# Second block: gate projections of the attention branch ahead of the branch's output projection, and the branch's result multiplied by its gate straight out of PSUM

## The chip, the core and the metric

One core of one Trainium2 chip runs the whole program. The time is the device time of one execution in microseconds (us), the median of several runs. Four compute engines matter here: PE (matrix products), DVE (elementwise on vectors), ACT (elementwise, activation functions) and POOL. SP issues the DMAs. Each engine works through its own instructions in order and waits on semaphores for the others.

## What is computed

A model of one sequence of 256 tokens and width 1024. `first_block` has two layers with two feed-forwards each, a pooling mixer and a block attention. `second_block` follows with two branches side by side: a state-space branch (`_ssm_branch`) and a multi-head latent attention (`_mla_branch`). Only the second block is touched:

```python
proj = h @ w_in[l]
u_s, z_s, q_lat, kv_lat, k_rope, z_m, gl_s, gl_m = jnp.split(proj, split_at, axis=-1)
y_s = _ssm_branch(u_s, ...)
glu_a, glu_b = jnp.split(jax.nn.gelu(y_s) @ w_glu[l] + b_glu[l], 2, axis=-1)
y_s = ((glu_a * jax.nn.sigmoid(glu_b)) * jax.nn.silu(z_s)) @ w_br_ssm[l]
y_m = _mla_branch(q_lat, kv_lat, k_rope, positions, ...)
y_m = (y_m * jax.nn.silu(z_m)) @ w_br_mla[l]
merged = jax.nn.sigmoid(gl_s) * y_s + jax.nn.sigmoid(gl_m) * y_m
out = merged @ w_out[l]
x = x + gate[:, None] * _rmsnorm(out, g_post[l])
```

All of it is float32.

## The kernel before

**Weights come as a stream of units.** A unit is 128 partitions by 1024 floats, 512 KB: for a projection, the weights of 128 output columns. `PHASES` gives the order of the 391 units, and the host lays them out in DRAM in that order (`parts`). Each unit goes through four hands: SP loads it into one of four `land` slots (`load_unit`), ACT rounds it to the upper part `w_hi` (`split_hi`, L392), DVE takes the lower part `w_lo` as a difference (`split_lo`, L396), and PE multiplies. A full float32 product is three PE products per 128 rows: `w_hi` by the upper input, `w_hi` by the lower, `w_lo` by the upper (`products`, L404 to L406; 24 per unit and 256 tokens). `w_hi` and `w_lo` have four slots each, so ACT can round unit u only when PE has finished unit u - 4 (semaphore `used`).

**Results come out in two PSUM banks.** `column_unit` writes result tile o into `tiles[:, o % 2]`, and first waits (`wait_bank`) until the owner of tile o - 2 has taken that tile out. `TILES` names the owner of each tile: "a" is ACT, "d" is DVE. Owners count up `freed["a"]` or `freed["d"]`.

**The gate stretch** is the list `GATES`: 32 units that only project, in four groups of eight. Before, these are `zs` (steps 0 to 7: silu of z_s into `zs_t`), `brm` (8 to 15: the attention branch's output projection, copied into `mrg`), `glm` (16 to 23: sigmoid of gl_m into `gs_t`) and `gls` (24 to 31: sigmoid of gl_s into the same `gs_t`). I call them steps 0 to 31, and PE, ACT and DVE each have one loop over them:

- PE: `column_unit` of step i. After steps 2, 5 and 10 it also does `state_in` (the inputs of the state-space scan), and after steps 8, 14, 20 and 26 two calls of `state_out` (L1074, L1076), each time for one more pair of the eight groups of channels.
- ACT: takes out tile i (`evacuate`, L1270), then `ahead()` rounds the unit of step i + 4. After the `state_out` steps it computes the gelu of the two results (`gelu_tile`, L1501), and at steps 19 and 26 it rounds what has come back from DRAM (`gelu_hi`, L1505).
- DVE: `ahead()` splits the unit of step i + 4, in `glm` steps multiplies `mrg[:, n]` by `gs_t[:, n]` (L2178, both in SBUF), and at most steps has one of 16 parts of the scan (`ssm_part`). Per pair k of groups there are four parts: part 0 (L2139 to L2144: four products that read PSUM, then two sums within SBUF), parts 1 and 2 (L2149: eight scans each), part 3 (L2156 to L2161), which ends with `zz_done`. `state_out` of pair k waits for that `zz_done`. Pairs 0, 1, 2 and 3 end their part 3 in the DVE steps 6, 12, 18 and 24; PE asks for them after its steps 8, 14, 20 and 26.
- POOL: after `zz_done` of pairs 0 and 1 it builds a table of rotations for pairs 2 and 3 (`table_step`, six products L2237 to L2242).

A change of activation function may need another function table in ACT (ACT_TABLE_LOAD). Before the gate stretch ACT computes a silu over all of `zm` (L1494). After it follow the `glu`, `brs` and `out` phases; in `brs`, DVE multiplies each result straight out of PSUM by `gs_t[:, n]` (L2201) and adds `mrg`.

## Time and profile before

| what | us |
|---|---|
| median of 3 runs | 1294.92 |
| lowest and highest run | 1294.7, 1297.7 |
| the profiled execution, its own time | 1294.78 |
| its span, first to last instruction | 1292.9 |
| in the span: gate stretch on PE, steps 0 to 31 | 1070.4 to 1188.6 |
| PE busy (share of the span) | 1234.9 (96%) |
| DVE busy | 1084.9 (84%) |
| ACT busy | 670.6 (52%) |
| POOL busy | 167.1 (13%) |

The profiled execution took 1294.78 us, 1.9 us more than its span; what lies outside the span is launch and end. Its time is 0.1 us below the median. All times of rows are us from the start of the span. A row of the timeline has the start, the length, the engine, the line, the operation, what is written from what, and the count; in brackets stands how long the engine was idle before and what released it. Instructions of one engine overlap a little at their ends, so what one adds to a queue is the distance between starts, not its length.

### The profile page before, as it was taken

To read this page: it belongs to the slowest core of one execution; us is meant where nothing else is said; L and a number is where in the kernel's file an instruction comes from. 1 tells how busy PE (TensorE), PEld (TensorE's weight loads), DVE (VectorE), ACT (ScalarE), POOL (GpSimd) and SP (SyncE) were. 2 spreads that over 40 slices of the span, in tenths; PEclk is the share of its full clock that TensorE was granted. 3 is DMA by queue.
4 is the path that set the end of the run, shared out by engine and by line. 5 is a ranking of instruction groups with operands and counts; after the bars stand their busy time and mean duration, and the time that the engine had idled before them with its cause. 6 is when DMAs were issued, how large, how long until landed. Compare 5 with 4: busy or idle time off the path is not lost.

```text
span 1292.9 us, 26721 instructions
## 1 busy us (share of the span) xinstructions
PE 1234.9 (96%) x10504; PEld 1205.2 (93%) x10504; DVE 1084.9 (84%) x1673; ACT 670.6 (52%) x1130; POOL 167.1 (13%) x195
## 2 busy tenths in 40 slices
PE   2999999899999999999999999999999999999996
PEld 1999999799999988999999999999999989999996
DVE  6998988898888877989989788999987577995584
ACT  2543434554444555664457664444465665455453
POOL 4599900000000000000001000000000022410000
PEclk8999999999999999999999999999999999999999
DMA  9999887489888459988853399887665898555561
GB/s 362 385 332 320 309 318 271 168 309 327 311 315 292 146 194 361 322 313 308 316 202 115 115 311 323 299 305 247 215 196 180 135 154 185 160 163 182 181 194 50
DMA packets 110926, 319.75 MB, mean 247 GB/s; under 512 B 24096, under 2 KB 35808, under 8 KB 110560
## 3 DMA queue, kind: packets, MB, share of 16 engines
q1 hardware_dynamic: 110816, 318.23, 74.0%
q8 instruction: 75, 1.23, 0.4%
q14 instruction: 35, 0.29, 0.1%
HBM read 313.18 MB, written 5.01 MB: 246 GB/s over the span
## 4 chain that ended last, share of the span: by engine, by line
PE 78%; DVE 12%; ACT 3%; DMA 3%; issue 2%; SPq 2%; ACTq 0%; DVEq 0%
PE quad L404 16%; PE quad L406 16%; PE quad L405 16%; PE acc L404 8%; PE acc L406 7%; PE acc L405 7%; DVE w_lo L396 3%; DVE arena L1572 2%; ACT w_hi L392 1%; PE quad L581 1%; PE quad L607 1%; DMA arena<-in_ssm_bw 1%; PE quad L609 1%; DMA land<-in_stream 1%; DMA x<-in_x_t 1%
## 5 line engine op out<-in xcount | busy, mean ns | idle before, releaser
L392 ACT CAST w_hi<-land 128x1024 fp32r<-128x1024 f32 x391 | 409.4, 1049 | 352.3 <-PE quad L406 239.3
L396 DVE TENSOR_TENSOR w_lo<-land,w_hi 128x1024 fp32r<-128x1024 f32 x391 | 485.1, 1246 | 118.5 <-ACT w_hi L392 116.2
L404 PE MATMUL quad<-xs_hi,w_hi 128*128 128x256 f32 (+1 forms) x1384 | 391.9, 283 | 0.8 <-DVE arena L2101 0.5
L406 PE MATMUL quad<-xs_hi,w_lo 128*128 128x256 f32 (+1 forms) x1384 | 390.0, 282 | 0.0
L405 PE MATMUL quad<-xs_lo,w_hi 128*128 128x256 f32 (+1 forms) x1384 | 389.4, 281 | 0.0
L404 PEld LDWEIGHTS quad<-xs_hi,w_hi 128*128 128x128 f32 x1384 | 260.8, 188 | 3.1 <-issue 0.9
L405 PEld LDWEIGHTS quad<-xs_lo,w_hi 128*128 128x128 f32 x1384 | 261.8, 189 | 0.1
L406 PEld LDWEIGHTS quad<-xs_hi,w_lo 128*128 128x128 f32 x1384 | 261.3, 189 | 0.0
L1572 DVE SCALAR_TENSOR_TENSOR arena<-arena 128x1024 f32<-128x1024 f32 x184 | 226.8, 1239 | 11.9 <-ACT arena L1295 8.4
L404 PE MATMUL acc<-h_hi,w_hi 128*128 128x256 f32 x704 | 196.9, 280 | 1.7 <-DVE h_lo L1622 1.3
L406 PE MATMUL acc<-h_hi,w_lo 128*128 128x256 f32 x704 | 196.7, 279 | 0.0
L405 PE MATMUL acc<-h_lo,w_hi 128*128 128x256 f32 x704 | 196.5, 279 | 0.0
L404 PE MATMUL quad<-as_hi,w_hi 128*128 128x258 f32 (+1 forms) x648 | 184.1, 284 | 1.2 <-DVE arena L2089 0.8
L406 PE MATMUL quad<-as_hi,w_lo 128*128 128x258 f32 (+1 forms) x648 | 182.1, 281 | 0.0
L405 PE MATMUL quad<-as_lo,w_hi 128*128 128x258 f32 (+1 forms) x648 | 182.0, 281 | 0.0
L404 PEld LDWEIGHTS acc<-h_hi,w_hi 128*128 128x128 f32 x704 | 132.2, 188 | 2.4 <-DVE w_lo L396 1.9
L406 PEld LDWEIGHTS acc<-h_hi,w_lo 128*128 128x128 f32 x704 | 132.4, 188 | 0.0
L405 PEld LDWEIGHTS acc<-h_lo,w_hi 128*128 128x128 f32 x704 | 132.3, 188 | 0.0
L404 PEld LDWEIGHTS quad<-as_hi,w_hi 128*128 128x128 f32 x648 | 122.3, 189 | 2.1 <-ACT arena L1270 0.7
L405 PEld LDWEIGHTS quad<-as_lo,w_hi 128*128 128x128 f32 x648 | 122.6, 189 | 0.1
L406 PEld LDWEIGHTS quad<-as_hi,w_lo 128*128 128x128 f32 x648 | 122.2, 189 | 0.0
L2329 POOL TENSOR_TENSOR arena<-arena,cons 128x256 f32<-128x256 f32 x8 | 6.6, 826 | 547.4 <-ACT arena L1359 545.7
(356 smaller groups left out, 1622.3 us busy)
## 6 DMA issues: line engine op xcount, KB each, us to landing
land<-in_stream SPq DMA_DIRECT2D x391, 512.0 KB, 4.4
arena<-in_gstream SPq DMA_DIRECT2D x184, 512.0 KB, 6.2
w_dram<-arena SPq DMA_DIRECT2D x3, 512.0 KB, 5.5
arena<-w_dram SPq DMA_DIRECT2D x6, 256.0 KB, 11.0
arena<-in_c_rows SPq DMA_DIRECT2D x2, 512.0 KB, 5.3
x<-in_x_t SPq DMA_DIRECT2D x1, 1024.0 KB, 9.5
arena<-in_ssm_bn SPq DMA_DIRECT2D x1, 1024.0 KB, 5.3
u_dram<-arena SPq DMA_DIRECT2D x1, 1024.0 KB, 5.3
```

Of the source, the lines that this page charges most:

```text
L392: nc.scalar.copy(w_hi[:, u % RING], land[:, u % LAND]).then_inc(hi_done, 1)
L396: nc.vector.tensor_tensor(w_lo[:, u % RING], land[:, u % LAND], w_hi[:, u % RING].bitcast(F32), ALU.subtract).then_inc(lo_done, 1)
L404: nc.tensor.matmul(outs, lh, rh, start=first, stop=False, **kw)
L405: nc.tensor.matmul(outs, lh, rl, start=False, stop=False, **kw)
L406: last = nc.tensor.matmul(outs, ll, rh, start=False, stop=end, **kw)
L581: m = nc.tensor.matmul(nrm[:, 0:T], ones, t_buf[:, k], start=(k == 0), stop=(k == KT - 1))
L607: nc.tensor.matmul(outs[c], lh, hi[:, k], start=(k == 0 and c in fresh), stop=False, skip_group_check=True)
L609: nc.tensor.matmul(outs[c], ll, hi[:, k], start=False, stop=False, skip_group_check=True)
L1572: V.scalar_tensor_tensor(out=rows, in0=rows, scalar=1.0, in1=c_rows[vector], op0=ALU.mult, op1=ALU.mult, accum_out=mods[:, bass.ds(i * 8 + ...
L2329: G.tensor_tensor(q_cos[:, h % 2], qT[:, h], cos1, ALU.mult).then_inc(q_cosd, 1)
```

## The change

The four groups of the gate stretch are put in the order `glm`, `brm`, `zs`, `gls`. The sigmoid of gl_m is now ready before the attention branch's results come, and these are no longer copied by ACT: their tiles belong to DVE, which multiplies them out of PSUM by `gs_t` into `mrg`. The separate product in the `glm` steps is gone, its semaphore `glm_done` too. `gls` writes `gs_t` again once DVE has freed the `brm` tile of the same number. `zs_t` and `gs_t` change places in SBUF, since `zm` is still being read when `glm` begins. The weight stream on the host is reordered to match; SP's, POOL's and PE's instructions are the same but for the semaphore that PE waits for before some tiles.

```diff
-          ("lat", 4), ("kr", 1), ("u", 6), ("qup", 4), ("kvup", 4), ("u2", 2), ("zm", 8), ("zs", 8), ("brm", 8),
-          ("glm", 8), ("gls", 8), ("glu", 16), ("brs", 8), ("out", 8)]
+          ("lat", 4), ("kr", 1), ("u", 6), ("qup", 4), ("kvup", 4), ("u2", 2), ("zm", 8), ("glm", 8), ("brm", 8),
+          ("zs", 8), ("gls", 8), ("glu", 16), ("brs", 8), ("out", 8)]
...
-         ("u", 6, "a"), ("qup", 8, "d"), ("kvup", 12, "a"), ("u2", 2, "a"), ("att2+zm", 16, "x"), ("zs", 8, "a"),
-         ("brm", 8, "a"), ("glm", 8, "a"), ("gls", 8, "a"), ("glu", 16, "y"), ("brs", 8, "d"), ("out", 8, "a")]
+         ("u", 6, "a"), ("qup", 8, "d"), ("kvup", 12, "a"), ("u2", 2, "a"), ("att2+zm", 16, "x"), ("glm", 8, "a"),
+         ("brm", 8, "d"), ("zs", 8, "a"), ("gls", 8, "a"), ("glu", 16, "y"), ("brs", 8, "d"), ("out", 8, "a")]
...
-GATES = [(_name, _n) for _name in ("zs", "brm", "glm", "gls") for _n in range(KT)]
+GATES = [(_name, _n) for _name in ("glm", "brm", "zs", "gls") for _n in range(KT)]
...
-        zs_t = region(40, [KT, T])
+        zs_t = region(16, [KT, T])
         mrg = region(48, [KT, T])
-        gs_t = region(16, [KT, T])
+        gs_t = region(40, [KT, T])
...
                 if nm == "zs":
                     evacuate(o, tile_of(nm, n), zs_t[:, n], ACT.Silu)
-                elif nm == "brm":
-                    evacuate(o, tile_of(nm, n), mrg[:, n])
-                else:
+                elif nm != "brm":
                     if nm == "gls":
-                        act.wait_ge(glm_done, n + 1)
+                        wait_freed(act, TILE["brm"] + n)
                     evacuate(o, tile_of(nm, n), gs_t[:, n], ACT.Sigmoid)
                 ahead()
...
             for i, (nm, n) in enumerate(GATES):
+                if nm == "brm":
+                    wait_tile(dve, TILE["brm"] + n)
+                    wait_freed(dve, TILE["glm"] + n)
+                    V.tensor_tensor(mrg[:, n], tiles[:, (TILE["brm"] + n) % 2, 0:T], gs_t[:, n],
+                                    ALU.mult).then_inc(freed["d"], 1)
                 ahead()
...
-                if nm == "glm":
-                    wait_freed(dve, TILE["glm"] + n)
-                    V.tensor_tensor(mrg[:, n], mrg[:, n], gs_t[:, n], ALU.mult).then_inc(glm_done, 1)
```

ACT at the start of the gate stretch and from step 24 on. L1270 is `evacuate`, L392 `split_hi`, L1494 the silu over `zm`:

```order
 L1494 ACT_TABLE_LOAD
 L1494 ACTIVATE arena<-arena 128x8x256 [waits freed_a]
+L1270 ACT_TABLE_LOAD
 L1270 ACTIVATE arena<-quad 128x256 [waits used]
 L392 CAST w_hi<-land 128x1024 [waits used,landed3]
```

A table load has come in behind the silu, since step 0 is a sigmoid now.

```order
-L1270 ACTIVATE arena<-quad 128x256 [waits used,glm_done]
-L392 CAST w_hi<-land 128x1024 [waits used,landed3]
...
+L1270 ACT_TABLE_LOAD [waits used]
+L1270 ACTIVATE arena<-quad 128x256 [waits freed_d]
+L392 CAST w_hi<-land 128x1024 [waits used,landed3]
```

At step 24 (silu to sigmoid, the first `gls` tile) a table load has come in that itself waits for PE's tile.

DVE, steps 13 to 16, before. L396 is `split_lo`, L2139 to L2144 part 0 of pair 2, L2149 scans, L2178 the product within SBUF:

```order
L2161 TENSOR_TENSOR arena<-arena 128x8x63
L396 TENSOR_TENSOR w_lo<-land,w_hi 128x1024 [waits hi_done] x2
L2139 TENSOR_TENSOR arena<-acc4,rope_tab 128x512 [waits bu_done,tab_done,zz_done]
...
L2144 TENSOR_TENSOR arena<-arena 128x512
L396 TENSOR_TENSOR w_lo<-land,w_hi 128x1024 [waits hi_done,dve_s]
L2149 SCALAR_TENSOR_TENSOR arena<-ssm_s,arena 128x64 x8
L396 TENSOR_TENSOR w_lo<-land,w_hi 128x1024 [waits hi_done,dve_s]
L2178 TENSOR_TENSOR arena<-arena 128x256 [waits freed_a]
```

No product stands here before step 16. And after (lines are 2 lower; L2173 is the new product out of PSUM):

```order
L2159 TENSOR_TENSOR arena<-arena 128x8x63
L2173 TENSOR_TENSOR arena<-quad,arena 128x256 [waits freed_a,used]
L396 TENSOR_TENSOR w_lo<-land,w_hi 128x1024 [waits hi_done]
L2173 TENSOR_TENSOR arena<-quad,arena 128x256 [waits freed_a,used]
L396 TENSOR_TENSOR w_lo<-land,w_hi 128x1024 [waits hi_done]
L2137 TENSOR_TENSOR arena<-acc4,rope_tab 128x512 [waits bu_done,tab_done,zz_done]
...
L2142 TENSOR_TENSOR arena<-arena 128x512
L2173 TENSOR_TENSOR arena<-quad,arena 128x256 [waits freed_a,used,dve_s]
L396 TENSOR_TENSOR w_lo<-land,w_hi 128x1024 [waits hi_done]
L2147 SCALAR_TENSOR_TENSOR arena<-ssm_s,arena 128x64 x8
```

Three products now stand in steps 13, 14 and 15, each ahead of the split of its step; the one of step 15 stands behind the whole of part 0. From step 16 on there is none.

## Rows read from the trace of the kernel before

**Rows 1.** The page: busy time by engine (1) and the chain that ended last (4).

```profile
PE 1234.9 (96%) x10504; PEld 1205.2 (93%) x10504; DVE 1084.9 (84%) x1673; ACT 670.6 (52%) x1130; POOL 167.1 (13%) x195
...
PE 78%; DVE 12%; ACT 3%; DMA 3%; issue 2%; SPq 2%; ACTq 0%; DVEq 0%
```

**Rows 2.** Windows: us, busy us (count) of PE, PEld, DVE, ACT, POOL, PEclk, DMA share, GB/s.

```profile
1097.00:1150.00 53.00, 49.78 (x606) 48.83 (x606) 49.67 (x86) 26.20 (x41) 18.51 (x12) 1.00 0.56 169
```

**Rows 3.** Waits of 1095 to 1195: who <- releaser: us in total, times, longest.

```profile
ACT arena L1270 <- PE quad L406: 43.5, 25, 3.7
...
PE quad L1074 <- DVE arena L2161: 4.1, 4, 1.7
```

**Rows 4.** Timeline, PE, first product of pairs 2, 3: start, us, what, [idle <-releaser].

```profile
1149.56 0.27 PE L1074 MATMUL quad<-arena 64*64 64x64 f32 x1 [1.67 <-DVE arena L2161]
...
1170.94 0.27 PE L1074 MATMUL quad<-arena 64*64 64x64 f32 x1 [0.91 <-DVE arena L2161]
```

**Rows 5.** Timeline, ACT, steps 0 and 1 of the gate stretch.

```profile
1070.40 1.28 ACT L1494 ACT_TABLE_LOAD   x1
1071.69 1.92 ACT L1494 ACTIVATE arena<-arena 128x2048 f32<-128x2048 f32 x1
1073.52 0.38 ACT L1270 ACTIVATE arena<-quad 128x256 f32<-128x256 f32 x1
1080.63 1.04 ACT L392 CAST w_hi<-land 128x1024 fp32r<-128x1024 f32 x1 [6.72 <-DMA land<-in_stream]
```

**Rows 6.** Timeline, ACT, steps 12 and 16.

```profile
1120.98 0.39 ACT L1270 ACTIVATE arena<-quad 128x256 f32<-128x256 f32 x1 [1.55 <-PE quad L406]
1121.26 1.04 ACT L392 CAST w_hi<-land 128x1024 fp32r<-128x1024 f32 x1
...
1136.51 0.39 ACT L1270 ACTIVATE arena<-quad 128x256 f32<-128x256 f32 x1 [0.24 <-PE quad L406]
```

**Rows 7.** Timeline, DVE, steps 12 to 17.

```profile
1122.40 1.23 DVE L396 TENSOR_TENSOR w_lo<-land,w_hi 128x1024 fp32r<-128x1024 f32 x1 [0.24 <-ACT w_hi L392]
...
1126.66 0.68 DVE L2161 TENSOR_TENSOR arena<-arena 128x504 f32<-128x504 f32 x1
1127.25 3.23 DVE L396 TENSOR_TENSOR w_lo<-land,w_hi 128x1024 fp32r<-128x1024 f32 x2
...
1132.90 1.57 DVE L2143 TENSOR_TENSOR arena<-arena 128x512 f32<-128x512 f32 x1
1134.40 1.56 DVE L2144 TENSOR_TENSOR arena<-arena 128x512 f32<-128x512 f32 x1
1135.99 2.19 DVE L396 TENSOR_TENSOR w_lo<-land,w_hi 128x1024 fp32r<-128x1024 f32 x1
...
1139.69 1.23 DVE L396 TENSOR_TENSOR w_lo<-land,w_hi 128x1024 fp32r<-128x1024 f32 x1
1140.84 0.42 DVE L2178 TENSOR_TENSOR arena<-arena 128x256 f32<-128x256 f32 x1
1141.17 1.22 DVE L396 TENSOR_TENSOR w_lo<-land,w_hi 128x1024 fp32r<-128x1024 f32 x1
```

**Rows 8.** Timeline, POOL, first and fourth of the six table products.

```profile
1127.47 1.92 POOL L2237 TENSOR_TENSOR cons<-base_t,chunk_t 128x512 f32<-128x512 f32 x1 [14.00 <-DVE arena L2161]
...
1132.86 1.07 POOL L2240 TENSOR_TENSOR cons<-base_t,chunk_t 128x512 f32<-128x512 f32 x1
```

**Rows 9.** Line L2201, a product that reads PSUM: count, min/median/max ns, first and last start.

```profile
L2201 DVE TENSOR_TENSOR arena<-quad,arena x8: 414/424/425, 1239.9 to 1257.7; 128x256 f32<-128x256 f32 x8
```

**Rows 10.** Timeline, ACT, step 24.

```profile
1164.43 0.39 ACT L1270 ACTIVATE arena<-quad 128x256 f32<-128x256 f32 x1 [1.59 <-PE quad L406]
1164.71 1.04 ACT L392 CAST w_hi<-land 128x1024 fp32r<-128x1024 f32 x1
```

**Rows 11.** Timeline, DVE, step 24.

```profile
1165.96 1.23 DVE L396 TENSOR_TENSOR w_lo<-land,w_hi 128x1024 fp32r<-128x1024 f32 x1
```

**Rows 12.** Timeline, ACT, step 27.

```profile
1177.25 1.28 ACT L1270 ACT_TABLE_LOAD   x1 [1.71 <-PE quad L406]
```

More of the change, by code:

```diff
@@ L341, in build_program @@
         y_done, gel_done, gv_done = sem("y_done"), sem("gel_done"), sem("gv_done")
-        zm_done, glm_done = sem("zm_done"), sem("glm_done")
+        zm_done = sem("zm_done")
         zero_cols = sem("zero_cols")
@@ L537, in _ @@
                     sp.dma_start(u2[r:r + 16], u_rows[g, t]).then_inc(u_in, 16)
-            for u in range(UNIT["zm"] + 6, UNIT["zs"] + 4):
+            for u in range(UNIT["zm"] + 6, UNIT["glm"] + 4):
                 load_unit(sp, u, u % LAND)
@@ L547, in _ @@
                     sp.dma_start(ba2[r:r + 16].rearrange("p j r n -> p j (r n)"), w_rows[g]).then_inc(ba_in, 16)
-            u = UNIT["zs"] + 4
+            u = UNIT["glm"] + 4
             for k in range(4):
-                while u < UNIT["zs"] + Y_AT[k] + 8:
+                while u < UNIT["glm"] + Y_AT[k] + 8:
                     load_unit(sp, u, u % LAND)
@@ L2443 @@
         columns(w_in2[:, 2592:3616]),
+        columns(w_in2[:, 4640:5664]),
+        columns(a["w_br_mla_2"][0]),
         columns(w_in2[:, 1024:2048]),
-        columns(a["w_br_mla_2"][0]),
-        columns(w_in2[:, 4640:5664]),
         columns(w_in2[:, 3616:4640]),
```

## The prediction

> **What bounds the kernel now.** I read the page first: PE is busy for 96% of the span, and the chain that ended last runs through PE for 78% and DVE for 12% [rows 1]. So a change of elementwise work can win only where PE stands still. The windows put the change's place, steps 6 to 20, at 53 us in which PE is busy for 49.8 and DVE for 49.7 [rows 2]: here DVE is as full as PE. The waits then say who waits: ACT's evacuations wait for PE, 43.5 us in total, so ACT has room; PE waits for DVE in four places, 4.1 us in total, always for L2161, the end of part 3 of the scan [rows 3]. The longest two are before `state_out` of pairs 2 and 3, 1.67 and 0.91 us [rows 4]. That is the whole prize in the gate stretch. Even if all four waits went, 4.1 us is 0.32% of 1294.9; 0.3% (3.9 us) is about what a measurement of this kernel can tell from no change.
>
> **Eight copies off ACT.** Each was an evacuation of 0.39 us, which takes 0.28 us of ACT's queue (1120.98 to 1121.26) [rows 6]. ACT waits 1.55 us for PE ahead of it [rows 6], so by itself this gives nothing. What it does give: in steps 8 to 15 the rounding of the next unit starts as soon as PE is done, 0.28 us sooner. That counts only where DVE sits waiting for it. It does in step 12, where DVE's split starts at 1122.40 after 0.24 us of idling [rows 7]: that wait goes (see below).
>
> **A table load at step 0.** The silu over `zm` ends at 1073.5, the evacuation of tile 0 follows at 1073.52, and the rounding behind it waits 6.72 us for its unit's DMA until 1080.63 [rows 5]. A load of 1.28 us moves the evacuation to 1074.8. PE needs that bank for step 2, two units after its start of step 0 at 1070.4; a unit is 2.87 us of ACT's cycle (1.55 + 0.28 + 1.04 [rows 6]) when PE sets the pace, so at 1076.1. Cost 0; the cover is 1.3 us. Without it the price would be at most 1.28 us.
>
> **Eight products, from steps 16 to 23 to steps 8 to 15.** The new one reads PSUM. The nearest row is L2201, the same form: 424 ns [rows 9], against 0.42 for the old one within SBUF, which takes 0.33 us of the queue (1140.84 to 1141.17) [rows 7]. I take 0.33 for both. The Trainium skill (VectorE: DVE Perf Modes, the section on the TRN2 errata) gives a DVE operation that reads PSUM 120 fixed cycles against 58, which speaks against this change by 0.065 us an operation, an estimate from that page, 0.2 to 0.3 us in sum; the rows show 0.006, and they decide.
>
> Steps 8 to 11: DVE has idle time before step 12, so these four are free. In step 12 I put the queue together anew: DVE was free at 1122.16 (1122.40 less 0.24) and is so 0.28 earlier, since it waited for ACT in step 11 too: 1121.9. The product takes 0.33, the rounding is done by 1122.0 (1121.26 + 1.04 - 0.28), the split starts at 1122.2. Part 3 of pair 1 ends 0.2 us sooner: **-0.2** at the wait before pair 1, carried down DVE's queue.
>
> Steps 13 to 15: DVE now runs without a pause to step 20, so three more products add 3 x 0.33 = 1.0 us; steps 16, 17 and 18 lose three, -1.0. On paper that cancels before part 3 of pair 2. But here POOL is in the way. Its table products start 0.14 us behind L2161, the first takes 1.92 us where the fourth, while DVE reads PSUM, takes 1.07 [rows 8], and DVE's operations with both inputs in SBUF take 1.57, 1.56 and 2.19 us where they otherwise take 0.68 (L2161, nearly the size of the first two) and 1.23 [rows 7]: the two take turns, whole operations at a time, while DVE's PSUM readers pass freely (in the 2.4 us between the two splits, which end at 1130.5, and L2143 at 1132.90 there are four of them, 0.60 each). Before, a split began at 1127.25 and was first; now a product out of PSUM stands there, POOL gets its turn first, and the split waits for it. Turn by turn, at 1.1 us for POOL's and for a split, 0.6 for L2143 and L2144: POOL to 1128.3, split to 1129.4, product, POOL to 1130.4, split to 1131.5, four PSUM readers beside POOL to 1133.9; there DVE and POOL come within 0.1 us of each other. If L2143 is first it ends at 1134.6, POOL goes to 1135.7, and L2144 ends at 1136.3; if POOL is first, both start about one turn later, and L2144 ends at 1137.6. Before it was 1135.95. The product of step 15 stands behind it and frees its bank at 1136.6 to 1137.9. PE wants that bank for step 17, after tile 16, which is done at 1136.4 [rows 6] less the 0.2 won. **A new wait of PE, 0.4 to 1.7 us, before step 17.** Queued behind the product in DVE: the split for step 19, the scans, part 3 of pair 2.
>
> That wait is mostly covered, for PE waited 1.67 us for the same DVE queue before pair 2 anyway [rows 4]. If part 0 ends early (1136.3), DVE arrives up to 0.5 sooner at pair 2 than before; if it ends late (1137.6), the roundings of steps 17 and 18 (they need PE's tiles 17 and 18) also come late and DVE waits for them: up to 0.5 later. I take **0**, from -0.5 to +0.5, for the moment at which `state_out` of pair 2 starts (1149.56). Everything before it, the -0.2 included, is in that figure.
>
> **A table load at step 24.** Between pair 2 and pair 3 DVE loses five products, 1.65 us, and PE's wait before pair 3 was 0.91 [rows 4]. That looks like a gain. But at step 24 DVE started its split at 1165.96, and the rounding it needs had ended only at 1165.75 (1164.71 + 1.04) [rows 10, 11]. So DVE was 0.2 us from being bound by ACT, and a faster DVE gains 0.2 at most. And ACT now has the new load in just that place: after `zs` (silu) comes the first `gls` (sigmoid), and the order shows that the load itself waits for PE's tile. Step 27, where such a load stood already, shows it: 1.71 us of waiting for PE, and then 1.28 us of load in front of the evacuation [rows 12]. So evacuation, rounding, split and part 3 all shift by 1.28: rounding done at 1167.03, split at 1167.1 and not 1165.96, **+1.1 us** on PE's wait before pair 3 (0.91 becomes 2.0). Bounds: -0.2 if the load were hidden, +1.28. I take +1.1, since the rows around it leave no other order. Nothing later gives it back: the gelu results of pair 3 go through DRAM and are rounded after step 31, in ACT's order, and from there PE is busy without a gap.
>
> For the load the Trainium skill has a rule that speaks against the change (ScalarE: Activation LUTs, What ACT_TABLE_LOAD costs): 1283 ns of load plus about 1380 ns of drain, so one should group functions by table set. The row at 1070.40 shows 1.28, and the next activation starts 1.29 us later [rows 5]: no drain. By the rule the load at step 24 would cost 2.66, an estimate from that page.
>
> **Sum.** 0 (step 0) + 0 (up to pair 2) + 1.1 (pair 3) = +1.1 us. The span goes from 1292.9 to 1294.0, the profiled execution from 1294.78 to 1295.9. It was 0.1 below the median, so the median goes from 1294.92 to **1296.0**.
>
> **Rivals.**
> A, *the load is hidden and the products pay*: DVE saves its five products and the 0.5 of the early end of part 0; PE's waits before pairs 2 and 3 shrink by 0.5 and 0.2: -0.7, 1294.2. For it: DVE is the releaser in all four waits. Against: the load stands in the chain of step 24.
> B, *it does nothing*: the copies and products were beside PE's work, and DVE and ACT trade equal parts: 1294.9. For it: 96% busy PE. Against: the same load.
> C, *slower by a feedback*: call X the end of the product of step 15. PE's tile 17 ends at X + 2.9, tile 18 at X + 5.7; its rounding is done 1.4 later, DVE's split 1.2 after that and part 3 of pair 2 another 3.7: pair 2 can start at X + 12.0. Up to X = 1137.6 this is no later than the 1149.56 of before, so PE's new wait costs nothing in the end; past it every us counts in full. If POOL gets two turns more than I count (1.3 us), X is 1139.2 and the price +1.6: with the load +2.7, 1297.6. From X = 1140.4 on it is slower by over 0.3%: 2.8 + 1.1 = +3.9, 1298.8. For it: DVE is full from 1122.4 on [rows 2, 7]. Against: POOL has six products in all.
> D, *the load costs more than its row*: the activation behind it starts late by as much as the load takes, another 1.28 [rows 12] on top of 1.1 at step 24: 1297.3. Against: the load at 1070.40, whose activation starts 1.29 later [rows 5]. The page's rule above is this rival, with 1.38 for the 1.28.
>
> **Chances.** Forecast, between +0.4 and +1.9: 0.62. A 0.10, B 0.12, C 0.12 (a third of it past 0.3%), D 0.04. The range reaches from just below A to the middle of C: 1293.9 to 1298.3. Faster by over 0.3% would need 3.9 us out of 4.1 of waits: 0.02. Slower by over 0.3%: 0.05, from C. Within: 0.93.
>
> **What would show it.** In the profile of the changed kernel: PE's idle times before pairs 0 and 1 together 0.2 below the 1.5 of now (4.1 less 1.67 less 0.91); a PE row at step 17 that waits for L2173; less than 1.67 before pair 2, with its start within 0.5 of 1149.56; an ACT_TABLE_LOAD at step 24 with an idle time before it, released by PE; about 2.0 us before pair 3. I am wrong if the stretch from pair 2 to pair 3 grows by less than 0.5 us, if PE waits at any step 9 to 16 for a bank, or if the time moves by more than 3 us either way.

## The result, and the profile after

| | kernel before | changed kernel |
|---|---|---|
| median, 11 runs each | 1295.07 | 1299.80 |
| lowest and highest run | 1293.46, 1297.70 | 1296.67, 1302.69 |
| profiled execution, its own time | 1294.78 | 1299.19 |
| its span | 1292.9 | 1297.4 |

The ratio is 1.0032, with a 95% interval of 1.0022 to 1.0042: 4.2 us by the ratio, 4.7 by the two medians. The forecast of 1296.0 is too low by 3.8 us, and its range ended at 1298.3. A repetition (below) gave 1.0022.

The page of the changed kernel, engines and chain, to lay beside [rows 1]:

```profile
PE 1237.9 (95%) x10504; PEld 1208.0 (93%) x10504; DVE 1084.5 (84%) x1673; ACT 671.2 (52%) x1124; POOL 167.5 (13%) x195
...
PE 82%; DVE 10%; ACT 3%; issue 2%; DMA 2%; SPq 1%; ACTq 0%; DVEq 0%
```

PE is busy 3.0 us longer with the same 10504 products, so some of them ran slower. The windows say where (us, busy us and count of PE, PEld, DVE, ACT and POOL, then PEclk, DMA share, GB/s). First the changed kernel, then the kernel before:

```profile
440.00:450.00 10.00, 7.83 (x51) 7.81 (x52) 9.19 (x20) 6.06 (x16) 0.00 (x0) 0.83 0.35 109
1053.00:1059.00 6.00, 6.00 (x40) 5.80 (x37) 4.68 (x9) 2.80 (x10) 0.00 (x0) 0.72 0.36 122
1097.00:1153.00 56.00, 52.43 (x625) 51.28 (x625) 52.69 (x94) 23.02 (x32) 18.20 (x12) 1.00 0.56 166
```

```profile
440.00:450.00 10.00, 8.13 (x61) 7.85 (x62) 8.89 (x20) 6.12 (x16) 0.00 (x0) 1.00 0.34 109
1053.00:1059.00 6.00, 6.00 (x50) 5.31 (x49) 5.24 (x10) 3.88 (x11) 0.85 (x1) 1.00 0.40 119
```

The granted clock is 0.83 over ten us in the one and 1.00 in the other: 1.7 us of full clock are missing, in a part of the program that the change doesn't touch. The same happens at 1053. I call such a stretch, in which TensorE has 1.2 and not 2.4 GHz, a **half-clock piece**; 1.7 us missing at half clock is a piece of 3.4 us. In the gate stretch itself the clock is 1.00 in both [rows 2].

Because of these pieces the starts of the two traces can't be compared; distances can. The first product of each `state_out` pair, and PE's wait at step 17, in the changed kernel (the line of part 3's end is L2159 now), to lay beside [rows 4]:

```profile
1106.36 0.30 PE L1074 MATMUL quad<-arena 64*64 64x64 f32 x2 [0.82 <-DVE arena L2159]
```

```profile
1129.79 0.32 PE L1074 MATMUL quad<-arena 64*64 64x64 f32 x2 [0.63 <-DVE arena L2159]
```

```profile
1140.24 0.39 PE L404 MATMUL quad<-xs_hi,w_hi 128*128 128x256 f32 x1 [1.38 <-DVE arena L2173]
```

```profile
1152.65 0.32 PE L1074 MATMUL quad<-arena 64*64 64x64 f32 x2 [0.74 <-DVE arena L2159]
```

```profile
1175.21 0.33 PE L1074 MATMUL quad<-arena 64*64 64x64 f32 x2 [2.07 <-DVE arena L2159]
```

| distance between pairs, us | before | changed | difference |
|---|---|---|---|
| 0 to 1 | 23.52 | 23.43 | -0.09 |
| 1 to 2 | 22.17 | 22.86 | +0.69 |
| 2 to 3 | 21.38 | 22.56 | +1.18 |
| sum | 67.07 | 68.85 | +1.78 |

In two traces of each kernel these distances agree within 0.1 us. So the stretch costs **1.8 us**, not 1.1; and the medians show more than that. The spans of the two traces differ by 4.5 us: 2.5 lie ahead of pair 0, where the two pieces are, 1.8 between pairs 0 and 3, and 0.2 behind pair 3.

**Pair 3.** ACT from step 24 on, and the DVE split behind it, to lay beside [rows 10 to 12]:

```profile
1167.51 1.28 ACT L1270 ACT_TABLE_LOAD   x1 [1.57 <-PE quad L406]
1168.81 0.39 ACT L1270 ACTIVATE arena<-quad 128x256 f32<-128x256 f32 x1
1169.09 1.04 ACT L392 CAST w_hi<-land 128x1024 fp32r<-128x1024 f32 x1
```

```profile
1170.23 1.23 DVE L396 TENSOR_TENSOR w_lo<-land,w_hi 128x1024 fp32r<-128x1024 f32 x1 [1.56 <-ACT w_hi L392]
```

The load waits for PE, then stands ahead of evacuation and rounding, and DVE waits 1.56 us for the rounding. This is the forecast chain, row by row.

**Pair 2.** DVE from step 13 to 18 (L2173 is the product out of PSUM, L2141 and L2142 the sums of part 0, [rows 7]) and POOL's first two products [rows 8]:

```profile
1129.65 0.41 DVE L2173 TENSOR_TENSOR arena<-quad,arena 128x256 f32<-128x256 f32 x1
1129.99 2.04 DVE L396 TENSOR_TENSOR w_lo<-land,w_hi 128x1024 fp32r<-128x1024 f32 x1
1131.95 0.41 DVE L2173 TENSOR_TENSOR arena<-quad,arena 128x256 f32<-128x256 f32 x1
1132.28 1.75 DVE L396 TENSOR_TENSOR w_lo<-land,w_hi 128x1024 fp32r<-128x1024 f32 x1
...
1136.46 1.58 DVE L2141 TENSOR_TENSOR arena<-arena 128x512 f32<-128x512 f32 x1
1137.96 1.76 DVE L2142 TENSOR_TENSOR arena<-arena 128x512 f32<-128x512 f32 x1
1139.76 0.42 DVE L2173 TENSOR_TENSOR arena<-quad,arena 128x256 f32<-128x256 f32 x1
...
1144.75 1.23 DVE L396 TENSOR_TENSOR w_lo<-land,w_hi 128x1024 fp32r<-128x1024 f32 x1 [0.69 <-ACT w_hi L392]
...
1147.67 1.22 DVE L396 TENSOR_TENSOR w_lo<-land,w_hi 128x1024 fp32r<-128x1024 f32 x1 [0.22 <-ACT w_hi L392]
```

```profile
1129.88 1.07 POOL L2237 TENSOR_TENSOR cons<-base_t,chunk_t 128x512 f32<-128x512 f32 x1 [13.90 <-DVE arena L2159]
1131.03 1.93 POOL L2238 TENSOR_TENSOR rh<-base_t,chunk_t 128x512 f32<-128x512 f32 x1
```

POOL starts at 1129.88 and the split at 1129.99: POOL is first, as expected, and the split takes 2.04 us. The product of step 15 ends at 1140.18, PE's tile 17 starts at 1140.24 after 1.38 us of waiting. Then comes what the sum put at zero: DVE waits 0.69 and 0.22 us for the roundings of steps 17 and 18, which came late since PE's tiles did.

**Step 0.** ACT's load and evacuation, and the rounding that waits for its DMA, [rows 5]:

```profile
1076.58 1.28 ACT L1270 ACT_TABLE_LOAD   x1
1077.87 0.39 ACT L1270 ACTIVATE arena<-quad 128x256 f32<-128x256 f32 x1
1082.83 1.04 ACT L392 CAST w_hi<-land 128x1024 fp32r<-128x1024 f32 x1 [4.57 <-DMA land<-in_stream]
```

The load is covered: the wait for the DMA is 4.57 and not 6.72 us. The next instruction starts 1.29 us after it, so rival D falls here, and at step 24 (1167.51 to 1168.81) as well.

### The profile page after: what moved, and what is told of

Read it like the earlier page. It is cut to its first block, busy times and chain, and to the rows that moved or that the text cites. A ratio compares the mean times of both kernels' runs of the same rounds, so it can differ in the third digit from the quotient of the medians.

```text
span 1297.4 us, 26719 instructions
## 1 busy us (share of the span) xinstructions
PE 1237.9 (95%) x10504; PEld 1208.0 (93%) x10504; DVE 1084.5 (84%) x1673; ACT 671.2 (52%) x1124; POOL 167.5 (13%) x195
## 4 chain that ended last, share of the span: by engine, by line
PE 82%; DVE 10%; ACT 3%; issue 2%; DMA 2%; SPq 1%; ACTq 0%; DVEq 0%
PE quad L404 17%; PE quad L406 17%; PE quad L405 17%; PE acc L404 8%; PE acc L406 7%; PE acc L405 7%; DVE w_lo L396 3%; DVE arena L1570 2%; ACT w_hi L392 1%; PE quad L607 1%; PE quad L609 1%; PE quad L581 1%; DMA land<-in_stream 1%; DMA x<-in_x_t 1%; DVE x L1692 1%
## 5 line engine op out<-in xcount | busy, mean ns | idle before, releaser
L392 ACT CAST w_hi<-land 128x1024 fp32r<-128x1024 f32 x391 | 409.4, 1049 | 368.7 <-PE quad L406 250.1
L396 DVE TENSOR_TENSOR w_lo<-land,w_hi 128x1024 fp32r<-128x1024 f32 x391 | 484.1, 1243 | 120.2 <-ACT w_hi L392 117.9
```

Source lines behind the costliest of these rows:

```text
L392: nc.scalar.copy(w_hi[:, u % RING], land[:, u % LAND]).then_inc(hi_done, 1)
L396: nc.vector.tensor_tensor(w_lo[:, u % RING], land[:, u % LAND], w_hi[:, u % RING].bitcast(F32), ALU.subtract).then_inc(lo_done, 1)
```

## Experiments

All were timed in five rounds beside runs of the kernel before on the same chip. "Mean" is the difference of the means to that kernel in the same comparison (single runs scatter with a standard deviation of 1.7 us, so a mean of 12 runs is good to about 0.5 us); "clock" is the mean granted clock of the runs, that of the kernel before being 0.9909 to 0.9916; "sum" is the distance from pair 0 to pair 3.

| kernel | runs | ratio, 95% interval | mean, us | clock | sum, us |
|---|---|---|---|---|---|
| rep_before | 12 | 1.0003 (0.9993 to 1.0013) | +0.1 | 0.9917 | 67.07 |
| rep_after | 12 | 1.0022 (1.0011 to 1.0034) | +2.3 | 0.9908 | 68.77 |
| a_nowait | 12 | 1.0004 (0.9991 to 1.0016) | +0.9 | 0.9913 | 67.52 |
| a_actcopy | 8 | 1.0027 (1.0016 to 1.0038) | +3.2 | 0.9903 | 68.49 |
| a_fill | 11 | 1.0006 (0.9994 to 1.0018) | +0.5 | 0.9914 | 68.91 |
| b_delay | 12 | 1.0005 (0.9994 to 1.0015) | +0.9 | 0.9908 | 68.33 |
| b_defer | 12 | 0.9990 (0.9978 to 1.0003) | -1.2 | 0.9913 | 65.97 |
| b_delay2 | 12 | 1.0027 (1.0014 to 1.0041) | +4.0 | 0.9903 | 69.73 |
| b_delay2_fill | 11 | 1.0013 (1.0002 to 1.0025) | +2.1 | 0.9916 | 69.71 |
| b_early | 11 | 1.0023 (1.0012 to 1.0034) | +2.5 | 0.9908 | 66.97 |
| b_best | 11 | 1.0016 (1.0005 to 1.0027) | +2.0 | 0.9917 | 65.96 |
| b_defer_fill | 12 | 1.0004 (0.9991 to 1.0018) | +0.6 | 0.9909 | 66.05 |
| b_fill442 | 12 | 0.9978 (0.9966 to 0.9989) | -2.7 | 0.9926 | 67.00 |
| b_defer442 | 6 | 0.9965 (0.9952 to 0.9978) | -3.4 | 0.9920 | 66.03 |
| a_442 | 12 | 1.0010 (0.9999 to 1.0021) | +1.1 | 0.9920 | 68.84 |
| a_442_fill | 12 | 0.9996 (0.9986 to 1.0007) | -0.2 | 0.9928 | 68.85 |

There were six comparisons, each with its own runs of the kernel before: rep_before to a_actcopy; a_fill to b_defer; b_delay2 to b_best; b_defer_fill; b_fill442 and b_defer442; a_442 and a_442_fill.

### Both kernels again (rep_before, rep_after)

> The kernel before, once more, for a second trace and for its spread beside the kernel after on one chip. Theory T1 (the change itself costs 1.8 us in the gate stretch, 1.38 before step 17 partly covered and 1.2 before pair 3; the other 2.5 us of the two traces lie ahead of the gate stretch in code that is the same, where TensorE ran at half clock for 443 to 447 and 1053 to 1059 us in the trace of after and not in that of before, and that is chance of a run): the distance from state_out of pair 0 to that of pair 3 is again 67.1 us, while the arrival at pair 0 (1103.9) may move by 2 us or more. Theory T2 (the half-clock pieces come with the changed kernel): no such pieces here, arrival within 0.5 us of 1103.9.

> The changed kernel, once more. Both theories: pair 0 to pair 3 again 68.9 us. T1: the half-clock pieces near 443 and 1053 us are there or not by chance, arrival at pair 0 between 1103.5 and 1108, ratio to before 1.001 to 1.003. T2: both pieces are there again, arrival at 1106.4, ratio 1.003 to 1.004.

The kernel before against itself is 1.0003. The changed one is 1.0022 and not 1.0032: of the 4.2 us that the ratio of the first comparison gives, some 1 to 2 were chance. Over all runs, 23 of the changed kernel have a mean of 1299.35 at a clock of 0.9905, 163 of the kernel before in the later comparisons 1296.49 at 0.9914: **2.9 us**, give or take 0.9. The stretch explains 1.8 of them. Among the 163 runs of the kernel before a run is 1.1 us longer for each 0.001 that its clock is lower; by that slope the clock of the changed kernel, 0.0009 lower, is worth 1.0. That slope is a correlation, and the mean clock is no pure count of pieces: it also holds the half clock at the start of the span, which lasts 10.2 us in 11 of the 18 traces and 13.7 in seven, whatever the kernel. What is left to find is why the clock of the changed kernel is lower.

### Without the wait that holds the table load (a_nowait)

```diff
-                    if nm == "gls":
-                        wait_freed(act, TILE["brm"] + n)
```

> The changed kernel without ACT's wait for the freed brm tile before each gls tile (PE's order already implies it), so that the table load of step 24 carries no wait and can be done while ACT idles ahead of PE's tile. If the load in the chain makes the 1.18 us between pairs 2 and 3: that distance falls from 22.56 to 21.3 (21.38 before), PE's wait before pair 3 from 2.07 to 0.7 or less, and the time is 1.2 us below that of the changed kernel. Rival (DVE or the DMAs make it, not the load): the distance stays at 22.5 and the time does not move.

The sigmoid's instruction then has one wait (for PE), and the load in front of it none. ACT at step 24 in a_nowait:

```profile
1164.76 1.28 ACT L1270 ACT_TABLE_LOAD   x1
1166.27 0.38 ACT L1270 ACTIVATE arena<-quad 128x256 f32<-128x256 f32 x1 [0.23 <-PE quad L406]
```

The load runs while ACT would wait for PE. The distance from pair 2 to pair 3 is 21.23 us, 1.33 shorter than in the changed kernel and even 0.15 shorter than before. So the load makes the whole +1.18 of pair 3, and only since it stands behind the wait.

### Copies by ACT, products within SBUF, in the new order (a_actcopy)

```diff
-("brm", 8, "d")
+("brm", 8, "a")
...
+                elif nm == "brm":
+                    evacuate(o, tile_of(nm, n), mrg[:, n])
...
-                    V.tensor_tensor(mrg[:, n], tiles[:, (TILE["brm"] + n) % 2, 0:T], gs_t[:, n],
-                                    ALU.mult).then_inc(freed["d"], 1)
+                    V.tensor_tensor(mrg[:, n], mrg[:, n], gs_t[:, n], ALU.mult).then_inc(glm_done, 1)
```

> The changed kernel with the brm tiles copied out by ACT again, as before, and multiplied by DVE within SBUF in the same steps 8 to 15: the new order, without a PSUM bank held by DVE. If the held bank makes the loss between pairs 1 and 2 (22.86 against 22.17): PE's wait of 1.38 before step 17 goes, and the distance falls to 22.2 to 22.5. Rival (DVE's longer queue beside POOL makes it, and the bank only shows it): the wait before step 17 goes, but the wait before pair 2 grows by as much and the distance stays at 22.8. The load at step 24 stays, so pair 2 to pair 3 is 22.5 in both.

DVE in steps 14 and 15 of a_actcopy, and PE at pair 2:

```profile
1131.61 1.28 DVE L2174 TENSOR_TENSOR arena<-arena 128x256 f32<-128x256 f32 x1
...
1139.75 0.43 DVE L2174 TENSOR_TENSOR arena<-arena 128x256 f32<-128x256 f32 x1
```

```profile
1151.67 0.33 PE L1074 MATMUL quad<-arena 64*64 64x64 f32 x2 [1.75 <-DVE arena L2161]
```

The product within SBUF waits in turn with POOL (1.28 us; out of PSUM the one in its place took 0.41), and the product of step 15 comes just as late in DVE's queue (1139.75, that is 10.36 us after pair 1 starts on PE; in the changed kernel 9.97). But it holds no bank now. PE doesn't wait at step 17, waits 1.75 before pair 2 as before, and the distance from pair 1 to 2 is 22.28, 0.11 above before. So of the 0.69 of pair 2, 0.58 comes from the **held bank**: a late product delays PE's tile, this the rounding, this DVE. DVE being late is not enough. This counts from pair 1. That pair itself comes 0.13 us later than before in a_actcopy and 0.09 sooner in the changed kernel; from pair 0 to pair 2 a_actcopy is 0.24 us longer than before and the changed kernel 0.60, so that the bank's share is 0.36 there. The mean of a_actcopy doesn't show this gain (+3.2 against +2.3), which is within the scatter of eight and twelve runs.

That a two-input operation within SBUF takes turns with POOL and a reader of PSUM does not is what the Trainium skill says (SBUF — State Buffer, Who interferes with whom: the shared port pair is an exclusive lock, and issue order decides who blocks); the rows agree, 1.28 against 0.41.

### Products deferred (b_defer)

```diff
+MERGE_AT = {19: (0,), 20: (1,), 21: (2,), 25: (3, 4, 5, 6, 7)}
...
-                if nm == "glm":
-                    wait_freed(dve, TILE["glm"] + n)
-                    V.tensor_tensor(mrg[:, n], mrg[:, n], gs_t[:, n], ALU.mult).then_inc(glm_done, 1)
+                for m in MERGE_AT.get(i, ()):
+                    wait_freed(dve, TILE["glm"] + m)
+                    V.tensor_tensor(mrg[:, m], mrg[:, m], gs_t[:, m], ALU.mult).then_inc(glm_done, 1)
```

> The kernel before (old order, ACT copies) with DVE's eight products moved within the glm and gls steps: products 0, 1, 2 in steps 19, 20, 21, products 3 to 7 in step 25, behind part 3 of pair 3, where DVE idles for 6.7 us. If DVE's queue is what PE waits for at pair 2 and ACT's rounding what it waits for at pair 3: pair 1 to pair 2 falls from 22.17 to 21.2, pair 2 to pair 3 from 21.38 to 21.2, so -1.2 in all, and the time is 1.2 to 2 us below before. Rival: PE's own work fills the stretch, and the distances fall by less than 0.3.

This is the kernel before, with the products taken out of DVE's way to pair 2 only. PE at pairs 2 and 3 in b_defer:

```profile
1150.54 0.32 PE L1075 MATMUL quad<-arena 64*64 64x64 f32 x2 [0.75 <-DVE arena L2162]
```

```profile
1171.83 0.33 PE L1075 MATMUL quad<-arena 64*64 64x64 f32 x2 [0.80 <-DVE arena L2162]
```

The wait before pair 2 falls from 1.67 to 0.75 and the sum by 1.1 us, as expected. In the times that is 0.9990, which can't be told from no change by itself.

### Does a long wait before pair 3 bring half-clock pieces? (a_fill, b_delay, b_delay2, b_delay2_fill)

a_fill is the changed kernel with useless products in the wait before pair 3, b_delay the kernel before with two DVE products of part 3 of pair 3 done twice:

```diff
+                if f >= 2:
+                    pe.wait_ge(gel_done, f - 1)
+                if f == 6:
+                    for _ in range(8):
+                        nc.tensor.matmul(y_out[0][:, 0:P], ones, ident, start=True, stop=True)
                 if f % 2 == 0:
                     pe.wait_ge(zz_done, f // 2 + 1)
-                if f >= 2:
-                    pe.wait_ge(gel_done, f - 1)
```

The wait for `gel_done` moves ahead of the useless products, since they write where the results of the pair before stood; so it does in the other kernels with this filler.

```diff
+                    if k == 3:
+                        V.tensor_tensor(m0, v[:, 1], sn, ALU.mult)
+                        link(V.tensor_tensor(m1, v[:, 1], cs, ALU.mult))
```

> The changed kernel with eight useless 128-column float32 products on TensorE after step 26, while it would wait for pair 3 (their result is overwritten). The wait of about 2.07 us becomes work; the distances between the pairs stay (22.56 from pair 2 to pair 3). T1 (the change costs the 1.8 us of the distances, the rest is chance): the mean time stays that of the changed kernel, the mean granted clock 0.9905. T3 (a wait of over 2 us before pair 3 makes TensorE fall to half clock in some runs, near 1174 us as in the trace of a_actcopy): the mean clock goes up towards 0.9915 and the mean time falls by 1 us or more without a change in the distances.

> The kernel before with two products of part 3 of pair 3 done twice on DVE (the same values), some 1.2 to 1.3 us more in front of pair 3 and nothing else: the size of the loss that the table load of step 24 makes. T1: pair 2 to pair 3 goes from 21.38 to 22.6, PE's wait from 0.9 to 2.1, the mean time by +1.2, the mean clock stays at 0.9916. T3: the same distances, the mean time by +2 to +3, the mean clock to 0.991 or less, since some runs have a piece at half clock behind the longer wait.

a_fill shows the sum of the changed kernel without its excess; its mean is even 1.3 us less than the sum asks for, which the pieces behind pair 3 can't explain. b_delay's sum is 1.26 us longer and its mean +0.9, where +2 to +3 was expected with pieces and +1.2 without: no excess that could be told, though its trace has a half-clock piece behind pair 3. As this was unclear, the delay was doubled (b_delay2: three times each product) and put on the chip together with the same kernel with 15 fillers (b_delay2_fill).

> The kernel before, with the first two products of part 3 of pair 3 done three times (four more products of 0.68 us on VectorE, nothing left out). In b_delay two more products made the distance from pair 2 to pair 3 1.33 us longer, so here it should be 2.7 longer (24.1) and PE's wait before pair 3 about 3.6 us. If only the wait itself costs (theory W), the mean is 2.7 us above the kernel before of this call. If a wait past 2 us is in addition followed by a piece in which TensorE has the clock of 1.2 GHz (theory T3), such a piece stands behind pair 3 in the trace, the mean is 3.5 to 4.7 above, and the mean granted clock is below that of the kernel before by 0.0005 or more.

> b_delay2 with 15 useless products of 128 columns on PE ahead of the wait before pair 3 (0.22 us each by a_fill, 3.3 us together), which keep PE busy through most of the wait. The distance from pair 2 to pair 3 should be that of b_delay2 within 0.1 us. Theory W: the same mean as b_delay2 within 0.5 us and no difference in the clock. Theory T3: no piece at the low clock behind pair 3, mean 0.8 to 2 us below b_delay2, and the clock of the kernel before.

PE and its window behind pair 3, first b_delay2, then b_delay2_fill (L1067 is the filler):

```profile
1175.39 0.33 PE L1074 MATMUL quad<-arena 64*64 64x64 f32 x2 [3.55 <-DVE arena L2164]
```

```profile
1174.00:1180.00 6.00, 4.61 (x97) 4.50 (x97) 3.56 (x5) 0.95 (x3) 0.00 (x0) 0.73 0.30 90
```

```profile
1171.90 3.51 PE L1067 MATMUL quad<-cons 128*128 128x128 f32 x30
1175.61 0.32 PE L1076 MATMUL quad<-arena 64*64 64x64 f32 x2 [0.20 <-DVE arena L2166]
```

```profile
1174.00:1180.00 6.00, 5.79 (x119) 5.54 (x118) 3.79 (x5) 2.33 (x5) 0.00 (x0) 1.00 0.25 90
```

Both have the same sum within 0.02 us, so by the stretch alone they are equal. The one in which PE stands idle for 3.55 us has a PEclk of 0.73 behind it; the one in which PE is kept busy has 1.00, and its mean is 1.9 us lower and its clock 0.0013 higher.

What a piece costs there can be read from all 18 traces. From the start of pair 3 to the end of the span it is 121.97 to 122.21 us in the 14 traces without a piece behind pair 3, and 123.48 to 123.76 in the four with one (a_actcopy, b_delay, b_delay2, a_442): **1.3 to 1.8 us** a piece.

### The filler near 442 (b_fill442, b_defer442, a_442, a_442_fill)

Half-clock pieces near 442 stand in 9 of the 14 traces of kernels without a filler there, always at one idle time of PE, here in the changed kernel:

```profile
442.17 0.36 PE L607 MATMUL quad<-as_hi,w_hi 128*128 128x258 f32 x1 [2.56 <-DVE w_lo L396]
```

```diff
                 pe.wait_ge(shift_cols, 2 * (e + 1))
+                for _ in range(9 if f == 2 else 0):
+                    nc.tensor.matmul(quad[:, 0, 0:P], ones, ident, start=True, stop=True)
                 first_units(head_unit(f, 0), [quad[:, b, 0:T + 2] for b in range(3)], *late_in[f], KT * stage,
```

> The kernel before with 9 useless products of 128 columns on PE in the wait of 2.55 us that ends near 442 (in b_defer_fill 9 such products took 2.25 us, but stood at 246, behind another wait). Nothing is left out. Theory I (the idle time brings the pieces at 1.2 GHz): none near 442, mean granted clock above that of the kernel before by 0.0006 to 0.0012, mean 0.8 to 1.5 us below. Theory O (they come from elsewhere): a piece near 442 as often as before, same mean within 0.5 us. In both the wait before the products at 442 is 0.3 us or less.

> b_fill442 with the products of b_defer (the eight products behind each other's scans, distances from pair 0 to pair 3 of 66.0 us in sum and not 67.1). Theory I: 1.9 to 2.6 us below the kernel before of this call, ratio 0.998 to 0.9985. Theory O: 0.6 to 1.6 us below.

PE and the window in b_fill442 (L713 is the filler):

```profile
440.01 2.17 PE L713 MATMUL quad<-cons 128*128 128x128 f32 x18
442.52 0.39 PE L607 MATMUL quad<-as_hi,w_hi 128*128 128x258 f32 x1 [0.34 <-DVE w_lo L396]
```

```profile
440.00:450.00 10.00, 9.66 (x76) 9.29 (x75) 9.75 (x22) 6.62 (x18) 0.00 (x0) 1.00 0.38 129
```

None of the four kernels with this filler has a half-clock piece there. It does no useful work and makes the kernel **2.7 us faster** (1.4 to 4.4 by the interval). With b_defer's edit on top (b_defer442) the ratio is 0.9965: this version beats both kernels. The traces explain less. Eight splits of DVE lie across this wait (from its 133rd to its 141st): they take 33.4 to 33.7 us in the nine traces with a piece, 32.1 to 32.2 in the five without, and 31.9 to 32.0 with the filler. So a piece costs 1.3 to 1.6 us, 9 of 14 of that is 1.0, and the filler gives 0.2 more. The other pairs that differ by this filler alone, from different comparisons, give 2.2 (b_defer442 and b_defer), 1.2 (a_442 and rep_after) and 0.7 us (a_442_fill and a_fill); all four together 1.9, give or take 0.8. What is above 1.2 isn't explained, and may be chance.

> The changed kernel with the 9 useless products of b_fill442 in the wait near 442. b_fill442 gained 2.7 us on the mean of the kernel before; the same here. Against the kernel before of this call: -2.7, +1.8 for the distances (total 68.8), and by theory T3 (a piece at 1.2 GHz behind the wait of 2.07 us in some runs) another +0.5 to +1.3: mean -0.4 to +0.4. If the rest was chance (theory W): mean -0.9 within 0.5. Mean clock by T3 below the 0.9926 of b_fill442 by 0.0004 or more, by W the same.

> a_442 with the 8 useless products of a_fill ahead of the wait before pair 3, distances as in a_442 within 0.1 us. Theory T3: mean 0.5 to 1.3 us below a_442 and a clock above it by 0.0004 or more; theory W: the same mean and clock. Both: -0.9 against the kernel before of this call, no piece at 1.2 GHz behind 1170.

a_442 and a_442_fill are the changed kernel with that filler, without and with the one of a_fill. Their windows behind pair 3:

```profile
1174.00:1180.00 6.00, 6.00 (x108) 5.93 (x105) 1.55 (x2) 1.76 (x4) 0.00 (x0) 0.76 0.36 98
```

```profile
1174.00:1180.00 6.00, 6.00 (x98) 5.93 (x95) 0.95 (x1) 2.73 (x5) 0.00 (x0) 1.00 0.44 122
```

At sums of 68.84 and 68.85 the means differ by 1.2 us and the clocks by 0.0008, as expected with pieces; both means are some 0.7 us above what was expected, in keeping with the filler near 442 giving less than 2.7. Taken with the other two pairs of the same kind (b_delay2 and b_delay2_fill 1.9; rep_after and a_fill, from two comparisons, 2.3 less 0.5), keeping PE busy in the wait before pair 3 gives 1.6 us, give or take 0.8. Against b_fill442, which has the same filler near 442, a_442_fill is 2.6 us longer and a_442 3.8, with 1.8 from the sum: of the 2.0 us of a_442 above the stretch, the filler before pair 3 takes away 1.2, within a scatter of about 1 us. In the traces, of six with a wait of 2.07 us or more before pair 3 four have a half-clock piece behind it (a_actcopy, b_delay, b_delay2, a_442; not the first trace of the changed kernel nor rep_after's); of twelve with less, none. Four of six at some 1.5 us a piece would be 1.0 us on the average.

### Two attempts that failed (b_early; b_best, b_defer_fill)

Another idle time, one that varies, stands in the attention, near 1051 (L796, PE waits for ACT's copy L1291). ACT's queue ahead of it in rep_before, then in b_defer, and PE there in b_defer:

```profile
1045.74 1.05 ACT L392 CAST w_hi<-land 128x1024 fp32r<-128x1024 f32 x1 [2.43 <-DMA land<-in_stream]
```

```profile
1048.28 1.04 ACT L393 CAST w_hi<-land 128x1024 fp32r<-128x1024 f32 x1 [4.46 <-DMA land<-in_stream]
```

```profile
1051.91 0.52 PE L797 MATMUL quad<-arena 128*64 128x256 f32 x2 [2.09 <-ACT arena L1292]
```

A rounding stands in front of ACT's exponentials and waits for weights that land now earlier, now later; PE waits 0 to 2.1 us, by chance. Behind waits of 1.88 to 2.10 a half-clock piece followed in five traces of six, behind shorter ones in none. b_early moves that rounding behind the copy:

```diff
-                if g:
-                    ahead()
+                if g:
+                    ahead({3: 0, 4: 2}.get(g, 1))
```

> The kernel before, with one rounding of the attention moved: the cast that waits for its weights from DRAM ahead of the exponentials of group 5 (2.4 to 4.5 us in nine traces, by chance) now comes behind the copy of group 4. Nothing is left out. In the traces PE's wait at L796 near 1051 was 0 to 2.1 us, the later that transfer landed the longer, and a piece at the low clock of TensorE followed in four of the five traces with a wait of 1.88 us or more. Theory S (this is one source of the spread between runs): the wait at L796 near 1051 is gone, the mean is 0.5 to 2.5 us below the kernel before and the standard deviation of the runs below its 1.7 us. Theory O (the spread comes from elsewhere): same mean within 0.5 us, same spread.

DVE and PE in b_early:

```profile
1050.31 1.23 DVE L396 TENSOR_TENSOR w_lo<-land,w_hi 128x1024 fp32r<-128x1024 f32 x1 [4.02 <-ACT w_hi L392]
```

```profile
1057.53 0.44 PE L796 MATMUL quad<-arena 128*64 128x256 f32 x2 [2.18 <-ACT arena L1291]
```

The wait near 1051 is gone, and one of 2.18 us stands at the next group: DVE now waits 4.02 us for the postponed rounding, with the maxima of the scores queued behind its split. The mean is 2.5 us worse, where 0.5 to 2.5 better was expected. The theory of the spread isn't refuted, but the edit only moved the wait. No half-clock piece follows the wait of 2.18, here or in b_best, so it doesn't explain the loss.

> The kernel before with three edits, nothing left out: the products of b_defer, the rounding of b_early, and 9 useless products of 128 columns on PE in its wait of 2.55 us near 440 (one of the places where a piece at 1.2 GHz followed in some traces). By b_defer -1.1 us (total of the distances from pair 0 to pair 3 66.0, not 67.1), by b_early 0.5 to 2.5, by the filler 0 to 1: mean 1.6 to 4.6 us below the kernel before, and no low clock near 442 in the trace. If the pieces near 442 don't come from the idle time ahead of them, they are seen here as often as elsewhere (four of nine traces) and the gain stays at 1.6 to 3.6.

> b_defer (the kernel before with its eight products behind each other's scans, steps 19 to 25) and the 9 useless products of 128 columns on PE in the wait of 2.55 us near 440, without the moved rounding of b_best; nothing is left out. In twelve traces of kernels without this filler a piece at 1.2 GHz followed near 442 in eight, in the one with it in none. A piece costs 1.5 to 2 us, so if the idle time is what brings it, the filler gains about 1.2 us on the mean of the runs: with the 1.1 of b_defer the mean is 1.5 to 3 us below the kernel before of this call, ratio 0.998 to 0.999, and the mean granted clock above its. If the pieces come from elsewhere, the mean is that of b_defer, 0.3 to 1.3 us below.

Both put the nine fillers into the wrong place, `f == 1` for `f == 2`. They stand behind a wait of 0.62 us at 246, as b_defer_fill shows, and the wait near 442 was left as it was, so the expectation of b_defer_fill, where it says "in the one with it in none", counts a trace of b_best in which that wait was not filled:

```profile
246.32 2.25 PE L714 MATMUL quad<-cons 128*128 128x128 f32 x18 [0.62 <-DVE x L1697]
```

So they measure b_defer plus 2.25 us of useless work in PE's way, and b_best in addition b_early's loss. That would be +1.0 and +3.6; measured are +0.6, in keeping with it, and +2.0, which is 1.6 less; they say nothing on the fillers near 442, which is why b_fill442 followed.

## Why the prediction was wrong

**Pairs 0 and 1: right in sign.** The waits before them are 1.45 together and not 1.55: 0.1 less, where 0.2 was expected.

**The held bank: right, and its price missed.** The new wait at step 17 is 1.38 us (0.4 to 1.7 expected), by the mechanism and the order of turns that the working called the late case. The step that failed is "I take **0**, from -0.5 to +0.5" for the start of `state_out` of pair 2: it is +0.6 from pair 0 on, +0.69 from pair 1. Rival C had the formula, pair 2 at X + 12.0. X is 1140.18, which is 1137.8 in the trace of before (pair 1 started 2.40 earlier there), and pair 2 started at X + 12.5. Half a us too little in a chain of roundings and splits, and the late case instead of the middle between both. a_actcopy shows that the bank makes most of this cost, 0.58 of the 0.69 from pair 1 and 0.36 of the 0.60 from pair 0, and DVE's lateness the rest.

**The load at step 24: right.** +1.18 where +1.1 was forecast, by the chain described; a_nowait takes it away.

**The load at step 0: right.** Covered.

**What the sum left out.** This is the second step that failed: the sum ended at the stretch and put PE's clock at nothing without a reason. Stretch and forecast differ by 0.7 us, the times by more. The wait before pair 3 went from 0.91 to the 2.0 that I had forecast myself, and what a wait of this length does to TensorE behind it, I didn't ask: in some runs it brings a half-clock piece: 1.0 us on the average by the clock of all runs, 1.0 by four of six traces at 1.3 to 1.8 us a piece, 1.6 by the fillers (0.8 to 2.4). Neither kept trace of the changed kernel itself has such a piece; the frequency comes from kernels with a wait of the same length or longer. The row in the trace of before was the idle time of 2.55 near 442; that trace has no half-clock piece behind it, and I took PE's clock as given. 1.8 + 1.0 = 2.8 of the 2.9 us of all runs; the 4.2 of the first comparison has in addition 1.3 us of chance, within its interval. With 2.9 us on the 1294.9 of the forecast the time would be 1297.8, inside the range: that the measured median lies beyond its end is that chance. That the forecast is too low is not.

**The test that the prediction set itself.** Of its marks the wait at step 17, the load behind an idle time of PE's making and the 2.0 us before pair 3 (2.07) came in, so did less than 1.67 us before pair 2 (0.74), and PE waits for no bank at steps 9 to 16. The start of pair 2 within 0.5 us and a move of the time by less than 3 us did not.

**The range and the chances.** Three runs from 1294.7 to 1297.7 were the only sign of the scatter. With single runs spread by 1.7 us the median of three is uncertain by about 1 us, and of eleven by half of that; the range counted only the mechanism's ends. So 0.93 for "within" and 0.05 for "slower" stood on a forecast of +1.1 with 2.8 us up to the bound and nothing on the way but rival C.

## What to carry to other kernels

When an engine's late result holds a PSUM bank, its lateness is paid by PE at once and comes back over the next roundings; the same lateness in SBUF costs less (here 0.24 and not 0.60 us). A function table load is hidden only where it need not wait itself: see whether the load or the instruction behind it carries the wait. And count an idle time of PE of some 2 us or more twice, for itself and for the slower products that may follow; useless products in it are worth a trial.

## What the runs showed of the hardware

TensorE dropped to 1.2 GHz for 3.4 us at a time in the middle of a kernel that is 96% busy. Between 45 and 1270 us of the 18 traces there are 23 such pieces, and each begins during or within 1.8 us of the end of one idle time of PE. They follow 20 of 31 idle times of 1.8 to 3.6 us, 3 of 50 of 1.4 to 1.8 us, and none of 11 of 1.0 to 1.4. The same idle time brings one in some runs and not in others (2.55 near 442: 9 of 14 traces). With nine useless products in that wait it did so in none of four. The Trainium skill has the mechanism (TensorE: Matmul & The Clock Gate, HAM oscillation: idle time between bursts of products throttles the array again, and the next burst starts cold); the rows agree that slower products follow idle time, but here single waits are enough, most of them shorter than those of its loop.

The shortest idle time with a piece behind it is the 1.45 us near 243 (b_delay, b_delay2_fill, b_fill442; L830 waits for DVE). PE in b_delay:

```profile
243.53 0.51 PE L830 MATMUL quad<-arena 128*128 128x144 f32 x2 [1.45 <-DVE x L1694]
...
247.86 0.64 PE L832 MATMUL quad<-arena 128*128 128x128 f32 x2
249.12 0.36 PE L607 MATMUL quad<-xs_hi,w_hi 128*128 128x258 f32 x1 [0.62 <-DVE x L1694]
```

The products are slow before the second wait, of 0.62 us, and so it is not what brings the piece. Near 1080 a piece follows 1.80 us of idling in rep_before and 2.12 in b_best, and none follows 1.91 in a_442_fill.

What decides whether a piece follows an idle time is open. So is whether the weights near 1047 land late by chance or through something in the kernel.
